# Twenty-four attention steps: gate products in two runs of fifteen and nine in place of three of nine, nine and six

## The reference, cut to what matters

```python
q, k, v, f, ga, gf = jnp.split(z, splits, axis=-1)          # z = h @ w_in
# diff_attention, per block of 128 queries and per head
s = einsum('bhcqd,bhckd->bhcqk', qi, k) * scale             # c = 0, 1
p = softmax(s)
a = p[:, :, 0] - lam * p[:, :, 1]
o = einsum('bhqk,bhkd->bhqd', a, v)
# then
o = rmsnorm(o, g_subln) * (1.0 - lam_init)
merged = sigmoid(ga) * (o @ w_pa) + sigmoid(gf) * (fm @ w_pf)
y = merged @ w_out
```

## Time and profile before

| | us |
|---|---|
| runs | 1936.02, 1935.08, 1940.41 |
| median of the runs | 1936.02 |
| profiled execution, its own time | 1939.63 |
| profiled execution, span from first to last instruction | 1937.8 |
| slots 6 to 29, the first scores at 248.12, the last turn at 413.07 | 165 |

### The profile page before, as it was taken

How to read it: one execution, slowest core, us unless ns; L and a number is a source line. 1 busy time by engine, 2 the same in 40 slices (tenths; PEclk the granted TensorE clock), 3 DMA queues, 4 the chain that set the end, 5 groups by cost and what they waited for, 6 DMA issues and landing times.

```text
span 1937.8 us, 36620 instructions
## 1 busy us (share of the span) xinstructions
PE 1893.7 (98%) x16561; PEld 887.0 (46%) x16561; DVE 498.7 (26%) x889; ACT 300.3 (15%) x547; POOL 145.6 (8%) x216
## 2 busy tenths in 40 slices
PE   6999999999979999999999999999999999999997
PEld 3899877779843333333333333333333333333332
DVE  2557456547260110111011011101101110110114
ACT  4322345443310000000000000000000000000001
POOL 2000000000120100001010000101000010100004
PEclk9999999999989999999999999999999999999999
DMA  8743111113579999999999999999999999999996
GB/s 348 277 186 143 60 36 66 35 62 120 230 273 405 413 420 411 419 414 411 420 413 420 412 418 414 412 420 413 419 412 419 410 412 420 413 411 411 416 409 280
DMA packets 101747, 644.50 MB, mean 333 GB/s; under 512 B 11840, under 2 KB 14288, under 8 KB 42976
## 3 DMA queue, kind: packets, MB, share of 16 engines
q1 hardware_dynamic: 94128, 618.23, 78.0%
q0 software_dynamic: 6608, 20.85, 3.4%
q10 hardware_dynamic: 864, 3.15, 0.4%
HBM read 625.66 MB, written 16.52 MB: 331 GB/s over the span
## 4 chain that ended last, share of the span: by engine, by line
PE 95%; DMA 2%; DVE 1%; POOL 1%; issue 0%; ACT 0%; SPq 0%; POOLq 0%; DVEq 0%; ACTq 0%
PE ps L932 93%; DMA m_half<-in_w_mod_rows 1%; PE ps L1113 1%; DMA out<-fin 1%; DMA x<-in_x_sample 0%; PE ps L1253 0%; PE ps L1035 0%; PE ps L940 0%; POOL rsx L773 0%; POOL rsx L772 0%; DVE Gs L1975 0%; DVE topi L2166 0%; PE ps L969 0%; DVE topv L2165 0%; PE ps L1143 0%
## 5 line engine op out<-in xcount | busy, mean ns | idle before, releaser
L932 PE MATMUL ps<-ring,xeT 128*32 128x512 f32 (+1 forms) x9216 | 915.3, 557 | 0.0
L932 PEld LDWEIGHTS ps<-ring,xeT 128*32 128x32 f32 x9216 | 299.0, 110 | 608.4 <-issue 607.2
L932 PE MATMUL ps<-ring,hidT 128*32 128x512 f32 x4224 | 459.7, 592 | 3.6 <-DMA ring<-in_w_dn 3.6
L932 PEld LDWEIGHTS ps<-ring,hidT 128*32 128x32 f32 x4224 | 137.0, 110 | 317.0 <-issue 310.0
L2304 DVE TENSOR_TENSOR hid<-sil,ps 128x768 f32<-128x768 f32 (+1 forms) x48 | 42.6, 888 | 915.7 <-ACT sil L1755 913.0
L1755 ACT ACTIVATE sil<-ps 128x768 f32<-128x768 f32 (+1 forms) x48 | 36.3, 757 | 960.5 <-PE ps L932 960.5
L932 PE MATMUL ps<-hT_hi,gq_hi 128*128 128x320 f32 x256 | 88.1, 344 | 0.0
L932 PE MATMUL ps<-in_hi,hT_hi 128*128 128x384 f32 x240 | 83.0, 346 | 2.5 <-ACT fT L1501 2.5
L932 PE MATMUL ps<-in_lo,hT_hi 128*128 128x384 f32 x240 | 81.0, 337 | 0.0
L932 PE MATMUL ps<-in_hi,hT_lo 128*128 128x384 f32 x240 | 81.0, 337 | 0.0
L860 POOL COPY idx_g<-idxT 128x1 int32 x42 | 13.7, 365 | 876.1 <-DVE xs L2286 876.1
(11 more groups left out here) (268 smaller groups left out, 1449.9 us busy)
## 6 DMA issues: line engine op xcount, KB each, us to landing
ring<-in_w_gu SPq DMA_DIRECT2D x256, 1024.0 KB
ring<-in_w_dn SPq DMA_DIRECT2D x176, 1024.0 KB
ring<-in_w_gu_rest SPq DMA_DIRECT2D x128, 768.0 KB
in_slab<-in_w_in_blocks SPq DMA_DIRECT2D x6, 1536.0 KB, 6.4
slab_y<-in_w_mod_blocks SPq DMA_DIRECT2D x4, 2048.0 KB, 10.4
m_half<-in_w_mod_rows SPq DMA_DIRECT2D x8, 1024.0 KB, 5.1
gq<-in_w_gates SPq DMA_DIRECT2D x16, 512.0 KB, 3.3
slab<-in_w_mod_blocks SPq DMA_DIRECT2D x3, 2048.0 KB, 16.4
```

The lines of the kernel that those rows point to most:

```text
L932: return pe.matmul(out, lhsT, rhs, start=first, stop=last, **kw)
```

## The change

In the 24 slots of latent items (6 to 29) the eight pieces of a slot are put in two parts in place of three. The number of pieces per slot, their order and everything else stay.

```diff
@@ -498,7 +498,7 @@
         SLOTS = NITEM + 4
         HT = TOK // 2
         PIECES = [(m, j, x, k) for m in range(KD) for j, n in enumerate((KD, KD, 2)) for x in range(2) for k in range(n)]
-        share = [(6, 6, 0) if i < 6 else (3, 3, 2) if i < NITEM else (6, 0, 0) for i in range(SLOTS)]
+        share = [(6, 6, 0) if i < 6 else (5, 3, 0) if i < NITEM else (6, 0, 0) for i in range(SLOTS)]
         first_piece = [sum(sum(x) for x in share[:i]) for i in range(SLOTS + 1)]
         assert first_piece[-1] == len(PIECES)
```

## The result

The changed kernel takes 1944.01 us (median of 7 runs, 1941.21 to 1945.08) against 1935.08 us (7 runs, 1934.04 to 1940.41): a ratio of 1.0042, with a 95% interval of 1.0033 to 1.0052, so 8.1 us slower. The forecast was 1942.7 us and slower by 6.7. The measured median lies 1.3 us above the forecast and inside the range of 1937 to 1948.

The account below looks back on a forecast made before the run. TensorE's stream was taken to bound the kernel. The terms 8.3 + 0.7 - 0.9 - 0.4 - 0.7 - 0.3 = +6.7 us, added to the median 1936.0, gave 1942.7 us, with a range of 1937 to 1948.

Parts of the forecast that it names:

- The bound: TensorE's stream, busy 98% of the span and 95% of the last chain: whatever lengthens it lengthens the kernel.
- What is moved where nothing waits: Six of 24 gate products moved from behind the second turn to ahead of the first: 1.10 us before, 1.08 after, nothing.
- The price per place: Squares or spread wait for ScalarE's copy at 12 places: 0.69 us each, priced from slot 30, 8.3 us in all.
- The tanh in front of the copy: ScalarE runs a half's tanh before the second turn's copy at six places: 0.12 us more each, 0.7 us.
- The gains: Savings from the longer first run and fewer joints, including -0.9 us in slot 7; bounds together 0 and about 3 us.
- The pairs of a second turn in 14 slots: Second turns just behind the first turn's copy take 0.18 us, not 0.13; the later turn removes this: -0.7 us.
- The first turns of slots 11, 15, 23 and 27: First turns slightly late where values stand; the longer first run saves 0.1 us each, -0.4 us.
- the joints of the Fourier pieces: One joint less between the two kinds of piece, in slots where Fourier pieces stand: -0.3 us for all.
- The copies were not hidden: Rival at the 12 places: copies stay hidden, only gains remain, -2.3 us, 1933.7 us; chance 0.09.
- ScalarE was not late by a tanh at each place: Rival: ScalarE late with a whole tanh, each of 12 places costs 1.13 us, +11.3 us, 1947.3 us; chance 0.13.
- The clock stayed at 1.00: Rival: uncovered waits bring TensorE to 1.2 GHz, 20 us on top of the 6.7, 1962.5 us; chance 0.03.
- The weight load's place: If the waiting product's weight load were pulled ahead, each place would cost some 0.05 us less, 7.7 for 8.3 us.

Follow-up runs that it names:

- e1: Changed kernel with three runs (nine, nine, six) kept in the twelve slots whose follower begins with squares or spread; 1937.52 us, 1.000 of the kernel before.
- e4: Changed kernel with a single wait left on squares and on spread, the one for o_rstd moved ahead of the second turn; 1943.09 us, 1.0033 of before.
- e5: Changed kernel with ScalarE's copy of the second turn put ahead of the tanh of a half that ended in part 1; 1943.36 us, 1.0037 of before.
- e3: Changed kernel with squares and spread moved behind the scores, VectorE's work on them behind its maxima; 1934.19 us, 0.9985 of before.
- e2: Changed kernel with fifteen and nine products only in the twelve slots whose follower begins with squares or spread, three runs elsewhere; 1943.78 us, 1.0037 of before.
- e7: e3 with slot 30's pieces put as three, two and one in place of six, none and none; 1933.21 us, 0.9981 of before.
- e6: Changed kernel with twelve, nine and three products in all 24 slots, so one piece behind the second turn; 1940.44 us, 1.002 of before.

## Why the prediction was right, point by point

- **The bound.** TensorE's stream held, and what is put into it comes out at the end: +7.9 us in the stretch, +8.1 in the ratio of the runs.
- **What is moved where nothing waits** was set at nothing. e1 shows it for the other twelve slots: -0.5 us, which is the pairs no longer held up (under the gains below): nine slots are shorter by 0.05 to 0.06 us each, and the three without such a pair are the same within 0.02.
- **The price per place**, 0.69 us, was the term that came out small. With one wait (e4) a spread costs just this, without a tanh: 0.747 from the last transpose less the 0.109 that it would take unhindered, and 0.05 for the slower start of the rest. For the squares the same count gives 0.74. And the second wait adds 0.06 to each. So 12 places cost 6 x (0.74 + 0.69) + 12 x 0.06 = 9.3 us, where 8.3 stood in the sum. The row of slot 30 was of the same transposes, copy and bank, but of a product with one wait; this I had not compared.
- **The tanh in front of the copy**: 0.12 us in six places forecast, 0.11 in six places measured, and taken away by e5.
- **The gains**: 2.3 us forecast. 9.3 + 0.7 - 7.9 leaves 2.1, and the traces account for 2.0 of it. Slot 7 lost 0.9 of its stall as worked out: fifteen products now stand in the 2.76 us that nine had (252.18 to 254.94; nine before). The pairs of a second turn in 14 slots, 0.15 to 0.17 from first to second transpose where they waited, are at 0.11 after: 0.75 us, for 0.7 forecast. The first turns of slots 11, 15, 23 and 27 give 0.08 each, 0.3 for 0.4. What is left for the joints of the Fourier pieces is 0.1, where 0.3 stood.
- **The rivals.** The copies were not hidden, and ScalarE was not late by a tanh at each place: the cost would have been 1.13 us, and was 0.75 to 0.80 without a tanh and 0.86 to 0.92 with one. The clock stayed at 1.00 through the stretch with twelve idle times of 0.5 to 0.7 us in it; the rule of the Trainium skill on such idle times ("TensorE: Matmul & The Clock Gate", "A second HAM failure mode: psum-queue depth-cycling") did not come to bear here.
- **The weight load's place.** In e4 the load of the waiting product starts with the product (288.70 both), as in slot 30. With two waits it starts 0.03 us ahead (287.06 and 287.09), after the copy's end at 286.94 all the same. The Trainium skill's rule that weight loads are pulled ahead of products in flight (same page, Part 2) hides nothing of such a wait in this kernel.

## What to carry to other kernels

Work used as filler between two dependent steps does its duty by where it stands: before it is moved, list for each place what it covers, a transpose's copy out of a bank as well as the long softmax chain, and who is the next user of that bank. The cure that worked here (e3) was to put something that uses other banks (the scores, 1.28 us) between the transpose and the bank's next user: the waits go, and the gain of the longer first run stays. Price an uncovered wait by a place in the same trace where it is uncovered already, and count the semaphores on the waiting instruction there and here.

## What the runs showed of the hardware that was not expected

A product with two waits started 0.53 us after the start of a copy of 256 columns, one with a single wait 0.43 us after it; with the faster following squares of the former the difference is 0.06 us net (e4).

The profiled executions of the two kernels differ by 1.6 us in span and their medians by 8.9. The same 25 products of each execution, from one router product to another, before and then after (columns as in rows 2; the counts take in products that reach over the edges):

```profile
529.24:535.86 6.62, 6.62 (x27) 5.73 (x27) 2.99 (x9) 3.07 (x6) 0.74 (x2) 0.50 0.10 41
```

```profile
534.07:537.84 3.77, 3.74 (x28) 3.04 (x27) 2.98 (x9) 2.16 (x6) 0.74 (x2) 1.00 0.24 102
```

TensorE was at 1.2 GHz (0.50) in the one and at 2.4 GHz (1.00) in the other. Both times router products of 16 columns stood right before. These 2.8 us are nearly the whole difference of the third stretch.

In the first stretch, before the change begins, the kernel before has the 3.3 us at 1.2 GHz of the earlier trace rows (12 products for 23, so 1.6 us), which are missing in the trace after; 1.3 of the 3.0 us are there already at the 101st product (32.70 against 31.40 us), and no run here shows where they come from. The other traces follow this: where no such low level lies ahead of slot 6 (after, e2, e7) its first scores come at 245.0 to 245.4, where one of 3.4 us does (before, e1, e3, e4, e5, e6) at 246.9 to 248.1, though no edit touches what lies ahead. A single pair of spans would have hidden four fifths of this change.
